# Feed-forward of a two-block model on one core: how the first product's sums are turned between partitions

## The reference

```python
for l in range(DEPTH):                      # DEPTH = 2
    ...                                     # mixers, output product, layer_norm
    f = jnp.square(jax.nn.relu(jnp.einsum('btd,df->btf', x, w_ff1[l])))   # 2048 -> 8192
    h = jnp.einsum('btf,fd->btd', f, w_ff2[l])                            # 8192 -> 2048
    x = layer_norm(DEEPNORM_ALPHA * x + h, ln2_g[l], ln2_b[l]).astype(dtype)
```

## Time and profile before

| | before |
|---|---|
| median of the runs (lowest, highest) | 3523.28 us (3523.19, 3527.66) |
| the profiled execution, its own time | 3518.38 us |
| its span, first to last instruction | 3516.6 us |
| mean granted TensorE clock | 0.994 |
| PE busy | 3434.2 us, 98% |
| DVE busy | 2158.6 us, 61% |
| ACT busy | 1631.8 us, 46% |
| POOL busy | 318.8 us, 9% |
| DMA, loads on SP's queue | 591.73 MB, 53.9% of 16 engines |
| loads of the feed-forward weights | 512 of 512 KB, 3.6 us from issue to landing |

### The profile page before, as it was taken

The page is one execution under the profiler, slowest core; times in us unless marked ns, Lnnn a source line. Parts: engine busy times, 40 slices in busy tenths (PEclk is TensorE's granted clock), DMA queues, the critical chain, the costliest instruction groups (busy, mean ns, idle before and its releaser), DMA issues.

```text
span 3516.6 us, 42994 instructions
## 1 busy us (share of the span) xinstructions
PE 3434.2 (98%) x16363; PEld 2867.1 (82%) x16363; DVE 2158.6 (61%) x2428; ACT 1631.8 (46%) x1988; POOL 318.8 (9%) x218
## 2 busy tenths in 40 slices
PE   8999999999999999989999999999999989999999
PEld 7788778888888787878788888888888879888877
DVE  6986665555555688865655555566446754656654
ACT  4544444444444346444544444444455654365553
POOL 0034000000000000340000000000000132000100
PEclk9999999999999999999999999999999999999999
DMA  7545565656565665446756565656655601565534
GB/s 235 180 143 163 179 198 188 190 190 192 185 193 186 188 198 156 144 150 197 240 191 189 188 191 188 189 181 209 184 178 175 202 6 35 192 189 174 180 120 162
DMA packets 312156, 617.05 MB, mean 175 GB/s; under 512 B 19353, under 2 KB 19353, under 8 KB 310315
## 3 DMA queue, kind: packets, MB, share of 16 engines
q1 hardware_dynamic: 306960, 591.73, 53.9%
q0 software_dynamic: 5024, 22.88, 2.0%
HBM read 612.44 MB, written 2.10 MB: 175 GB/s over the span
## 4 chain that ended last, share of the span: by engine, by line
PE 85%; DVE 9%; ACT 3%; POOL 1%; DMA 1%; issue 1%; SPq 0%; DVEq 0%; ACTq 0%; POOLq 0%
PE ps_unit L277 26%; PE ps_unit L279 26%; PE ps_unit L278 25%; DVE sb_w_lo L261 3%; DVE sb_conv_y L1218 2%; PE ps_mix L2677 2%; PE ps_mix L1292 1%; PE ps_mix L862 1%; ACT sb_w_hi L254 1%; PE ps_mix L2675 1%; DMA sb_raw<-in_w_in_dram 0%; PE ps_mix L305 0%; PE ps_mix L706 0%; DVE sb_x L436 0%; PE ps_mix L3054 0%
## 5 line engine op out<-in xcount | busy, mean ns | idle before, releaser
L261 DVE TENSOR_TENSOR sb_w_lo<-sb_raw,sb_w_hi 128x1024 fp32r<-128x1024 f32 x1120 | 1404.8, 1268 | 1014.0 <-ACT sb_w_hi L254 1010.6
L254 ACT ACTIVATE sb_w_hi<-sb_raw 128x1024 fp32r<-128x1024 f32 x1120 | 1176.7, 1059 | 1410.0 <-DMA sb_raw<-in_w_ff_dram 709.4
L277 PE MATMUL ps_unit<-sb_w_hi,sb_a_hi 128*128 128x512 f32 x3456 | 1365.6, 395 | 17.5 <-DVE sb_a_lo L748 13.3
L279 PE MATMUL ps_unit<-sb_w_hi,sb_a_lo 128*128 128x512 f32 x3456 | 1350.7, 391 | 0.0
L278 PE MATMUL ps_unit<-sb_w_lo,sb_a_hi 128*128 128x512 f32 x3456 | 1349.1, 390 | 0.0
L277 PEld LDWEIGHTS ps_unit<-sb_w_hi,sb_a_hi 128*128 128x128 f32 x3456 | 652.0, 189 | 154.8 <-DVE sb_a_lo L748 14.8
L279 PEld LDWEIGHTS ps_unit<-sb_w_hi,sb_a_lo 128*128 128x128 f32 x3456 | 651.1, 188 | 137.8
L278 PEld LDWEIGHTS ps_unit<-sb_w_lo,sb_a_hi 128*128 128x128 f32 x3456 | 652.2, 189 | 131.4
L277 PE MATMUL ps_unit<-sb_w_hi,sb_f_hi 128*128 128x512 f32 x1024 | 400.0, 391 | 0.0
L279 PE MATMUL ps_unit<-sb_w_hi,sb_f_lo 128*128 128x512 f32 x1024 | 398.6, 389 | 0.0
L278 PE MATMUL ps_unit<-sb_w_lo,sb_f_hi 128*128 128x512 f32 x1024 | 398.4, 389 | 0.0
(11 more groups left out here) (459 smaller groups left out, 2028.0 us busy)
## 6 DMA issues: line engine op xcount, KB each, us to landing
sb_raw<-in_w_ff_dram SPq DMA_DIRECT2D x512, 512.0 KB, 3.6
sb_raw<-in_w_in_dram SPq DMA_DIRECT2D x224, 512.0 KB, 3.6
sb_raw<-in_e_w_in_dram SPq DMA_DIRECT2D x112, 512.0 KB, 3.4
sb_raw<-in_o_w_in_dram SPq DMA_DIRECT2D x112, 512.0 KB, 3.6
sb_raw<-in_w_out_dram SPq DMA_DIRECT2D x64, 512.0 KB, 3.9
sb_raw<-in_e_w_out_dram SPq DMA_DIRECT2D x32, 512.0 KB, 3.4
sb_raw<-in_o_w_out_dram SPq DMA_DIRECT2D x32, 512.0 KB, 3.4
sb_raw<-in_e_w_mem_kv_dram SPq DMA_DIRECT2D x16, 512.0 KB, 3.7
```

The source lines that it names most:

```text
L254: k.nc.scalar.activation(k.w_hi[:, j], k.raw[:, j], ACT.Copy).then_inc(k.hi_ready, 1)
L261: k.nc.vector.tensor_tensor(k.w_lo[:, j], k.raw[:, j], k.w_hi[:, j].bitcast(F32), ALU.subtract).then_inc(k.lo_ready, 1)
L277: k.nc.tensor.matmul(acc, hi[:, kt, tokens], w_hi, start=kt == 0, stop=False)
L279: last = k.nc.tensor.matmul(acc, lo[:, kt, tokens], w_hi, start=False, stop=kt == KT - 1)
```

## The change

The sums are turned before Relu and square, without PE.
- DVE takes the unit's sums from PSUM in two transposes (one per token tile) into `f_out`. DVE's transpose turns each block of 32 x 32 within its 32 partitions. This frees the PSUM buffer (`evacuated`, now from DVE).
- SP moves 16 pieces of 32 partitions x 256 numbers (32 KB) from `f_out` to `f_in`, from partition block a to partition block b. It does so just before it issues the load of block (u, 0), for the sums of unit u - 2 (u = 2 to 5). Each of the four units has a semaphore of its own (`f_moved`).
- DVE computes max(x, 0) * x from `f_in` to `f_out` in one operation, in unit u for the sums of unit u - 1, behind its fourth split.
- ACT, behind its fifth split, writes `f_hi`, and DVE, behind its fifth split, `f_lo`, each in two operations with a reordering of runs of 32 numbers.
- POOL has no part any more, PE neither.

```diff
--- before.py
+++ after.py
@@ -140,8 +140,8 @@
     k.proj = sb("proj", k.p0, [P, TT, D_IN])
     k.f_hi = sb("f_hi", k.p0, [P, KT, SEQ], F32R)
     k.f_lo = sb("f_lo", k.p0 + 16 * K, [P, KT, SEQ], F32R)
-    k.relu = sb("relu", k.p0 + 32 * K, [P, 2, TT, NC])
-    k.relu2 = sb("relu2", k.p0 + 40 * K, [P, 2, TT, NC])
+    k.f_out = sb("f_out", k.p0 + 32 * K, [P, 2, TT * NC])
+    k.f_in = sb("f_in", k.p0 + 40 * K, [P, 2, TT * NC])
     t0 = 168 * K
     k.square = sb("square", t0, [P, 4, P])
     k.ident, k.tri, k.tri_t, k.ones = (k.square[:, n, :] for n in range(4))
@@ -183,8 +183,8 @@
     k.block_done = nc.alloc_semaphore("block_done")
     k.evacuated = nc.alloc_semaphore("evacuated")
     k.block0 = dict.fromkeys(("sp", "act", "dve", "pe", "pool"), 0)
+    k.f_moved = [nc.alloc_semaphore(f"f_moved{u}") for u in range(4)]
     k.relu2_ready = nc.alloc_semaphore("relu2_ready")
-    k.f_turned = nc.alloc_semaphore("f_turned")
     k.f_lo_ready = nc.alloc_semaphore("f_lo_ready")
     k.f_hi_ready = nc.alloc_semaphore("f_hi_ready")
     k.stats_ready = nc.alloc_semaphore("stats_ready")
@@ -828,6 +828,32 @@
 FF_UNITS = 2 * (D // NC)
 
 
+SQ = 32
+
+
+def turned_square(k, u, a, b):
+
+    part = TT * NC // 4
+    return k.f_out[a * SQ:(a + 1) * SQ, u % 2, b * part:(b + 1) * part]
+
+
+def moved_square(k, u, a, b):
+
+    part = TT * NC // 4
+    return k.f_in[b * SQ:(b + 1) * SQ, u % 2, a * part:(a + 1) * part]
+
+
+def feature_rows(k, u, t):
+
+
+    return k.f_out[:, u % 2, :].rearrange("p (a t m j) -> p t m a j", a=4, t=TT, m=4)[:, t]
+
+
+def feature_tokens(buffer, u, t):
+
+    return buffer[:, 4 * u:4 * u + 4, t * P:(t + 1) * P].rearrange("p m (a j) -> p m a j", a=4)
+
+
 def sp_feed_forward(sp, k, w1, w2):
     first = k.block0["sp"]
     k.block0["sp"] += FF_GROUPS * FF_UNITS * BLOCKS
@@ -838,6 +864,11 @@
         for u in range(FF_UNITS):
             for j in range(BLOCKS):
                 rows = slice(KB * j, KB * (j + 1))
+                if 2 <= u <= 5 and j == 0:
+                    sp.wait_ge(k.evacuated, b0 + (u + 1) * BLOCKS)
+                    for a in range(4):
+                        for b in range(4):
+                            sp.dma_start(moved_square(k, u - 2, a, b), turned_square(k, u - 2, a, b))                                .then_inc(k.f_moved[u - 2], 16)
                 if u < 4:
                     src = w1_rows[:, rows, bass.ds(q * D + u * NC, NC)]
                 else:
@@ -850,18 +881,6 @@
     first = k.block0["pe"]
     k.block0["pe"] += FF_GROUPS * FF_UNITS * BLOCKS
     done = layer * FF_GROUPS * 4
-
-    def turn(n, u):
-
-
-        pe.wait_ge(k.relu2_ready, n + (u + 3))
-        pe.wait_ge(k.f_lo_ready, n + (u + 1))
-        for kt in range(4):
-            bank = k.ps[:, 2 * (u % 2) + kt // 2, :].rearrange("p (a s) -> p a s", a=2)
-            for t in range(TT):
-                last = k.nc.tensor.transpose(bank[:, kt % 2, t * P:(t + 1) * P],
-                                             k.relu2[:, u % 2, t, kt * P:(kt + 1) * P], k.ident)
-        last.then_inc(k.f_turned, 1)
 
     def group(q, g0, between=None):
 
@@ -878,8 +897,6 @@
             for j in range(BLOCKS):
                 if u == 4 and j == 0:
                     pe.wait_ge(k.f_lo_ready, n + 5)
-                if j == 4 and 1 <= u <= 4:
-                    turn(n, u - 1)
                 if u == 4 and j == 6:
                     pe.wait_ge(k.f_lo_ready, n + 6)
                 if between:
@@ -889,10 +906,6 @@
     group(0, 0)
     for q in range(1, FF_GROUPS):
         group(0, q, between if q == FF_GROUPS - 1 else None)
-
-
-def turned_unit(k, u):
-    return k.ps[:, 2 * (u % 2):2 * (u % 2) + 2, :].rearrange("p b (a s) -> p (b a) s", a=2)
 
 
 def act_feed_forward(act, k, layer, between=None, root=None):
@@ -907,10 +920,6 @@
                 act_split(act, k, b0, u * BLOCKS + j)
                 if between:
                     between(u, j - AHEAD)
-            if 1 <= u <= 4:
-                act.wait_ge(k.f_turned, n + (u + 2))
-                k.nc.scalar.activation(k.f_hi[:, 4 * (u - 1):4 * u, :], turned_unit(k, u - 1),
-                                       ACT.Copy).then_inc(k.f_hi_ready, 1)
             if root and u == FF_UNITS - 1:
                 act_split(act, k, b0, u * BLOCKS + AHEAD + 4)
                 act_seam(act, k, b0, FF_UNITS * BLOCKS, root)
@@ -919,10 +928,11 @@
                 act_split(act, k, b0, u * BLOCKS + j)
                 if between:
                     between(u, j - AHEAD)
-            if u < 4:
-                wait_unit(act, k, b0, u)
-                act.wait_ge(k.relu2_ready, n + (u + 1))
-                k.nc.scalar.activation(k.relu[:, u % 2], k.ps_unit[:, u % 2], ACT.Relu).then_inc(k.evacuated, BLOCKS)
+                if 1 <= u <= 4 and j == AHEAD + 4:
+                    act.wait_ge(k.relu2_ready, n + u)
+                    for t in range(TT):
+                        last = k.nc.scalar.activation(feature_tokens(k.f_hi, u - 1, t), feature_rows(k, u - 1, t), ACT.Copy)
+                    last.then_inc(k.f_hi_ready, 1)
 
     def scale(u, j):
         if u == 1:
@@ -932,20 +942,6 @@
     with act.Fori(1, FF_GROUPS - 1) as q:
         group(q)
     group(FF_GROUPS - 1, between, root)
-
-
-def pool_feed_forward(pool, k, layer):
-    first = k.block0["pool"]
-    k.block0["pool"] += FF_GROUPS * FF_UNITS * BLOCKS
-    done = layer * FF_GROUPS * 4
-    with pool.Fori(0, FF_GROUPS) as q:
-        b0 = q * (FF_UNITS * BLOCKS) + first
-        n = q * 4 + done
-        for u in range(4):
-            pool.wait_ge(k.evacuated, b0 + (u + 3) * BLOCKS)
-            pool.wait_ge(k.f_turned, n + (u + 1))
-            k.nc.gpsimd.tensor_tensor(k.relu2[:, u % 2], k.relu[:, u % 2], k.relu[:, u % 2],
-                                      ALU.mult).then_inc(k.relu2_ready, 1)
 
 
 def dve_feed_forward(dve, k, layer, between=None, norm=None):
@@ -959,16 +955,17 @@
     def group(q, between=None, norm=None):
         b0 = q * (FF_UNITS * BLOCKS) + first
         n = q * 4 + done
+        m = q * 256 + layer * FF_GROUPS * 256
         for u in range(FF_UNITS):
             for j in range(AHEAD, AHEAD + 4):
                 dve_split(dve, k, b0, u * BLOCKS + j)
                 if between:
                     between(u, j - AHEAD)
             if 1 <= u <= 4:
-                dve.wait_ge(k.f_hi_ready, n + u)
-                part = slice(4 * (u - 1), 4 * u)
-                k.nc.vector.tensor_tensor(k.f_lo[:, part, :], turned_unit(k, u - 1), k.f_hi[:, part, :].bitcast(F32),
-                                          ALU.subtract).then_inc(k.f_lo_ready, 1)
+                dve.wait_ge(k.f_moved[u - 1], m + 256)
+                sums = k.f_in[:, (u - 1) % 2, :]
+                k.nc.vector.scalar_tensor_tensor(k.f_out[:, (u - 1) % 2, :], sums, 0.0, sums, ALU.max, ALU.mult)\
+                    .then_inc(k.relu2_ready, 1)
             if norm and u == FF_UNITS - 1:
                 dve_split(dve, k, b0, u * BLOCKS + AHEAD + 4)
                 dve_seam(dve, k, b0, u, u - 4, norm)
@@ -981,6 +978,22 @@
                 dve_split(dve, k, b0, u * BLOCKS + j)
                 if between:
                     between(u, j - AHEAD)
+                if 1 <= u <= 4 and j == AHEAD + 4:
+                    dve.wait_ge(k.f_hi_ready, n + u)
+                    for t in range(TT):
+                        last = k.nc.vector.tensor_tensor(feature_tokens(k.f_lo, u - 1, t), feature_rows(k, u - 1, t),
+                                                         feature_tokens(k.f_hi, u - 1, t).bitcast(F32), ALU.subtract)
+                    last.then_inc(k.f_lo_ready, 1)
+            if u < 4:
+
+
+                wait_unit(dve, k, b0, u)
+                dve.wait_ge(k.f_lo_ready, n + (u + 1))
+                for t in range(TT):
+                    out = k.f_out[:, u % 2, :].rearrange("p (b t m j) -> p t b m j", b=4, t=TT, m=4)[:, t]
+                    sums = k.ps_unit[:, u % 2, t, :].rearrange("p (m b j) -> p b m j", m=4, b=4)
+                    last = k.nc.vector.transpose(out, sums)
+                last.then_inc(k.evacuated, BLOCKS)
 
     with dve.Fori(0, FF_GROUPS - 1) as q:
         group(q)
@@ -3224,7 +3237,6 @@
 
         @block.gpsimd
         def _(pool):
-            pool.sem_inc(k.relu2_ready, 2)
             nc.gpsimd.memset(k.eps[:, 0:1], LN_EPS)
             nc.gpsimd.memset(k.eps[:, 1:2], EPS).then_inc(*k.eps_set.up())
             with nc.allow_non_contiguous_dma(reason="positions"):
@@ -3244,8 +3256,7 @@
                 if l == DEPTH - 1:
                     pool.dma_start(k.mem[:], tokens(d["mem_2"][0])).then_inc(*k.mem_in.up(16))
                     pool.dma_start(k.mem_gain[:], d["mem_norm_g_2"].partition_broadcast(P)).then_inc(*k.mem_in.up(16))
-                k.block0["pool"] += (IN_UNITS + OUT_UNITS) * BLOCKS
-                pool_feed_forward(pool, k, l)
+                k.block0["pool"] += (IN_UNITS + OUT_UNITS + FF_GROUPS * FF_UNITS) * BLOCKS
```

(1 more changed line is left out.)

## The result

The changed kernel takes 3715.16 us (median of four runs, 3714.3 to 3719.79); the kernel before, beside it, 3523.24 us (3519.45 to 3527.66). The ratio is 1.0552, 95% interval [1.0536, 1.0568]: 192 us slower. The forecast was 3558 us with a range up to 3600: the sign and the place of the loss were right, its size was missed by more than five times (35 us against 192).

The account below looks back on a forecast made before the run. PE, busy every microsecond, was taken as the bound. Per group, -3.5 us for four turns, +6.3 waiting for f_lo and +1.6 lost clock give +4.4; eight groups add 35 to 3523.3, so 3558 us, range 3498 to 3600.

Parts of the forecast that it names:

- The gain of 28 us: On PE, 32 turns of eight transposes each go away, at 0.88 us a turn.
- Step 1: On DVE, two 128x512 transposes of a unit's sums from PSUM take 1.3 us; bounds 1.2 and 2.5.
- the square: On DVE, Relu and square in one 128x1024 operation take 1.2 us.
- step 5: f_hi on ACT takes 1.2 us beside a DVE split, then f_lo on DVE 1.35 us.
- step 6: After f_lo, DVE does three splits and the next unit's transposes: 4.7 us.
- the loop through SP's queue: From one unit's f_lo to the next takes 22.6 us against PE's 21.75, slipping 0.9 us a unit within a group.
- step 2: On SP, 16 moves are issued in order ahead of load (u+2, 0): 0.42 us each, 6.7 us; bounds 5.9 and 7.7.
- Step 3: Loads (u+2, 0) and (u+2, 1) wait behind the 16 issues; the second lands 5.0 us after them.
- The weights themselves stay ahead: The split of (u+2, 0), at T+13 to 16 after the unit's end T on PE, is wanted only at T+21.75.
- The clock: On PE, about eight matmuls behind each long wait run at half clock, losing 1.6 us a group.
- Serial moves: Rival: each move lands before the next starts, at least 2 us each, 32 us a unit: +850 us; chance 0.03.
- Slow pieces on SP: Rival: 0.48 us an issue (or DVE pieces at twice the price), two waits a group, +66 to +72 us; chance 0.15.

Follow-up runs that it names:

- e1: Changed kernel without the 16 moves, the square reading the sums where the transposes left them: 3494.3 us against 3518.33 for the kernel before.
- e4: Changed kernel with each group's four units' moves replaced by four other transfer forms, only to read issue times; one execution, span 3619.1 us.
- e7: Changed kernel with the square reading f_out directly while SP still issues 16 same-size moves from a constant tile: 3711.44 us, ratio 1.0551 to the kernel before.
- e2: Changed kernel with eight moves of 64 KB instead of sixteen of 32 KB: 3554.89 us, ratio 1.0099 to the kernel before.
- e6: Changed kernel with the 16 moves on SP spread, four ahead of each of four loads: 3580.53 us, ratio 1.0173 to the kernel before.
- e10: Changed kernel, its 16 moves kept on SP, with square, f_hi and f_lo two splits earlier: 3644.75 us, ratio 1.036 to the kernel before.
- e5: Changed kernel with the moves replaced by one store to DRAM and four reads ahead of load (u+2, 1): 3540.88 us, ratio 1.0063 to the kernel before.
- e8: As e5, but the four reads stand ahead of load (u+2, 2): 3520.25 us, ratio 1.0001 to the kernel before.
- e9: Changed kernel with eight moves issued by GpSimd and eight by SP ahead of load (u+2, 2): 3522.46 us, ratio 1.0015 to the kernel before.
- e11: As e5, with square, f_hi and f_lo two splits earlier: 3490.64 us against 3517.56 for the kernel before, ratio 0.9927.

## Why the prediction was wrong, point by point

**What stood.** The gain of 28 us (e1: 24 us on the medians, 27.9 on the spans of two single executions). Step 1 (1.3 us for two transposes: 1.31), the square (1.2: 1.22), step 5 (`f_hi` 0.62 each, `f_lo` 0.685), step 6 (4.7: 4.6). The mechanism: the loop through SP's queue, ACT and DVE outlasts PE's unit, slips from unit to unit, and PE pays where it asks for `f_lo`. The Trainium skill, "VectorE: DVE Perf Modes", section "The three transpose paths", had led to an estimate of 0.71 us for a 128x512 transpose; the trace has 0.690.

**The step that failed is step 2,** "I take 0.42 each, 6.7 us; bounds 0.37 and 0.48". An issue with SBUF at both ends is 0.59, with the gap 0.625; sixteen are 10.0 us. All my rows were of loads from DRAM; I bounded the price by their spread and treated a form that the trace did not show as one that it did. The issues of e4 with the source in DRAM fall in those bounds (0.42), the others do not.

**Step 3 was short too**: from the end of the burst to the landing of (u+2, 1) took 5.8 us (724.97 to about 730.8), not 5.0: the first load behind the burst landed after 4.4 us, not 3.6. It is the smaller part: 0.8 against 3.3 us.

**What the two did to the sum.** The chain is 22.0 us instead of 17.9, the loop 26.6 instead of 22.6, the slip 4.9 us a unit instead of 0.9. With these in the prediction's own working, `f_lo` of unit 2 is at T+1.9+9.8+22.0 = T+33.7 and PE waits 12.0 us at (4, 0) where it was to wait none; `f_lo` of unit 3 is at T+38.6, and behind the first wait another 10.3 us are left at (4, 6). That is 22.3 us a group, 178 in eight. The trace has 145.1 us on `f_lo`, 9.4 and 8.7 at the two places, and 172.7 with the waits on weights, which put PE, and so the moment at which it asks, later. The prediction had 50.

**"The weights themselves stay ahead"** was wrong: 14 waits, 31.2 us. Behind 10 us of burst in each of four units the loads come crowded, and SP, ACT and DVE do not catch up in time.

**The clock.** 1.6 us a wait was forecast, with one wait a group (13 us in all). After a wait of 8.9 us it is 2.4; with 27 new waits (16 - 0 and 14 - 3) the sum is 51 us, 1.9 each. That the cost is the clock's is read from one stretch and from the balance; no run changed the clock by itself.

Together: 122 us more waiting and 38 more at the lower clock, on a forecast of 35, give 195; measured were 196 on the spans, 192 on the medians.

**The rivals.** Serial moves are excluded (the moves land 1.9 us after their issue, and e7 doesn't wait for them at all). "Slow pieces on SP" had the right place, but its worst figure, 0.48, ended the range at 3600. The prediction itself said that the sum leans 32-fold on each term of the loop; a range that ends 0.06 us above the value taken, for a form not seen, did not heed it. With 0.60 and the gap of 0.04 as the upper end it would have reached 16 x 0.22 x 32 = 113 us above the forecast, to 3671, and with two waits of clock a group beyond that.

**Two slips in the prediction's working** changed nothing. The split (u+1, 5), done at T+0.6, is wanted five blocks behind the unit's end, not six. And by its own terms waits of 4.5 to 8 us a group give +21 to +49 us, not +15 to +55.

**The size of a transfer.** The Trainium skill, "DMA: Bandwidth & Descriptors", section "Bandwidth", calls transfers under 64 KB descriptor-dominated. Here transfers of 32 and 64 KB cost the same issue (590 ns) and land after 1.9 and 2.0 us, so larger pieces do pay (e2 against the changed kernel), here by the issuing engine's time: the DMA engines were busy 58% in the window 600 to 700, and 29% while SP issued a burst (715 to 725).

**Left open.** Why an issue between two SBUF tiles is dearer was not settled; the runs show only where. How the loss splits between the two loads in front of the square and the six behind them was not tried apart from e6 to e10. Nor was it measured how much of the late landings (4 to 7 us instead of 3.6) in e2, e5, e8 and e9 is the extra traffic, and how much the loads that catch up.

## What to carry to other kernels

The price of a DMA on a shared in-order queue is the time that it keeps the queue from what stands behind it. List who waits, on every engine, for the next loads in that queue, and move the consumer out from behind them (e11), not the moves alone (e8). Count the time that is to be had from where the chain begins: in e2 it was 14.2 us from the transposes, not 16.3. Price an issue by a row with the same memories at both ends; where there is none, leave the range open by half its value, and where a chain is close to a loop's period, multiply that by the loops it slips through.

## What the hardware showed that was not expected

- An issue on SP takes 590 to 601 ns from SBUF to SBUF, whatever its shape (32x256, 32x512, 128x64, 128x256), 421 from DRAM to SBUF with 32 rows, 349 from SBUF to DRAM with 128 rows of 4 KB, 373 for the loads of 512 KB.
- From GpSimd the same moves take 496 ns each, less than on SP, but land 3.4 us after the issue instead of 1.9.
- A round trip through DRAM (in e5 the store landed after 3.9 us, the reads after 2.9) with five issues was faster for the kernel than sixteen direct moves (e5 3540.88 against 3715.16 us, e11 3490.64 against e10's 3644.75).
- Loads of 512 KB that land after 3.6 us when one is issued every 2.72 us took 4.3 to 7.2 us when eight were issued within 10.2 us behind a burst.
